# Order of the moving columns and place of the stationary buffers in a split-fp32 encoder trunk

## The chip, the cores and the metric

The kernel runs on one NeuronCore of a Trainium2 chip. The metric is device time of one launch in microseconds; 3 runs of the kernel before gave 2326.38, 2326.87 and 2327.36 us (median 2326.87).

## What is computed

One layer of an encoder trunk on 256 tokens of width 2048: half a SwiGLU FFN (width 5632), a mixing block in which a Conformer convolution (31 taps) and a 16-head latent attention work on the same normalised input and are merged by sigmoid gates, and a second half SwiGLU FFN. In outline:

```
x = x + 0.5 * swiglu_ffn(rms_norm(x, ffn1_norm_g), ffn1_w_gate, ffn1_w_up, ffn1_w_down)
u = rms_norm(x, mix_norm_g) @ w_in
y_conv = conformer_conv_branch(u_conv, ...) ; y_mla = mla_branch(c_q_raw, c_kv_raw, k_rope_raw, ...)
x = x + (sigmoid(gl_conv) * y_conv + sigmoid(gl_mla) * y_mla) @ w_out
x = x + 0.5 * swiglu_ffn(rms_norm(x, ffn2_norm_g), ffn2_w_gate, ffn2_w_up, ffn2_w_down)
return rms_norm(x, final_norm_g)
```

All of it is float32. The matrix products are by far the largest part, and nearly all are activations (256 tokens) times a weight matrix that is used once.

## The kernel before

**Units.** The weight matrices come from HBM in 814 units, one DMA each, issued by SyncE (L399). A unit of the wide stages holds two blocks (`DEEP = 2`) of 128 input channels by 512 output channels (`WIDE`), side by side in a partition: 128 partitions by 1024 floats. The host lays the weights out this way (`units_of`). 774 units are of this kind; 8 (the last group of the stage "latents") have blocks of 320 columns, and 32 belong to the attention heads, whose weights are laid out by another function (`head_units`).

**Rings.** A unit lands in one of four slots (`SLOTS`) of the ring `raw`. ScalarE rounds it to the reduced format fp32r into the ring `w_hi` (L432), VectorE writes the rest, raw minus rounded, into the ring `w_lo` (L927), and TensorE then multiplies. Activations are split into two such parts too and are kept whole in stationary buffers: `h`, `hidden`, `attn`, `merged`, `c_q` and `c_kv`.

**Products.** `wide_unit` does 12 matmuls for each unit: two blocks, two halves of the tokens, and three products each (`multiply`, L682 to L684: high by high, high by low, low by high). The stationary operand of each, loaded into the array by a LDWEIGHTS of its own, is 128 channels by 128 tokens of a stationary buffer; the moving operand is a block of 512 columns of `w_hi` or `w_lo`, read from the first column to the last; the result adds up in a PSUM bank. TensorE frees a slot with the last matmul of a unit (`unit_used`), and the three engines otherwise follow one another through counters (`hi_ready`, `lo_ready`), four units deep. In `head_pair` the queries and keys are made with the ring's weights as the stationary operand and `c_q` or `c_kv` moving (256 columns), the values with `c_kv` stationary and 256 columns of the ring moving. Attention scores and values (L799, L800, L825) and transposes (L693, L810, L879) are plain float32.

**Places.** In each partition the buffers lie one behind the other in the order in which they are declared. In the kernel before `w_hi` begins at byte 17536 and `w_lo` at 33920; `h` begins at 66688, `hidden` at 113792, `attn` and `merged` at 132224, `c_kv` at 197760 and `c_q` at 205952. Each of these is a multiple of 1024 bytes away from the others. A slot is 4096 bytes, a block of 512 columns 2048 bytes, a stationary block of 128 tokens 512 bytes.

Of the kernel before, what the change touches and what calls it, by code (L numbers as in the profile page):

```python
# [14 lines left out]
P = 128  # L15
# [19 lines left out]
WIDE = 512  # L35
DEEP = 2
SLOTS = 4
UNIT = WIDE * DEEP

AHEAD = SLOTS  # L40

# [122 lines left out]
def encoder(nc, streams, xt_in, x_in, pos_in, gains_in, final_in, taps_in, const_in, freq_in, out):  # L164
# [6 lines left out]
    with ExitStack() as ctx:  # L171
        def sb(name, shape, dt=F32, stack=ctx):
            return stack.enter_context(nc.sbuf_tensor(name, shape, dt))

        def sem(name):
            return ctx.enter_context(nc.semaphore(name))

        raw = sb("raw", [P, SLOTS, UNIT])
        w_hi = sb("w_hi", [P, SLOTS, UNIT], F32R)
        w_lo = sb("w_lo", [P, SLOTS, UNIT], F32R)  # L180
        x = sb("x", [P, 2, D])
        h = sb("h", [P, KT, 2, T], F32R)
        identity = sb("identity", [P, P])
# [91 lines left out]

        raw_loaded = [sem(f"raw_loaded{j}") for j in range(SLOTS)]
        xt_loaded = [sem(f"xt_loaded{j}") for j in range(KT // DEEP)]
# [60 lines left out]
        def banks(g):  # L338
            return bank[2 * g.pair], bank[2 * g.pair + 1]
# [51 lines left out]
        block = ctx.enter_context(nc.Block())  # L391

        @block.sync
        def _(sp):
            def load(u):
                stage, at, n = units[u]
                if u >= SLOTS:
                    sp.wait_ge(lo_ready, u + 1 - SLOTS)
# [278 lines left out]
        def _(pe):  # L677

            def multiply(dst, fixed, moving, first, last):
                fixed_hi, fixed_lo = fixed  # L680
                moving_hi, moving_lo = moving
                pe.matmul(dst, fixed_hi, moving_hi, start=first, stop=False)  # L682
                pe.matmul(dst, fixed_hi, moving_lo, start=False, stop=False)  # L683
                return pe.matmul(dst, fixed_lo, moving_hi, start=False, stop=last)  # L684
# [42 lines left out]
            def low_turned(stage, kinds, k):  # L727

                g = [g for g in plan.stage(stage) if g.kind in kinds][k // 4]
                t = turns[g.turn + k % 4 // 2]  # L730
                return t.lo_before + t.lo
# [19 lines left out]
            def wait_stationary(g, k):  # L751

                if g.stage == "ffn1_up":
                    pe.wait_ge(xt_lo, k + 2)
                elif g.stage in ("ffn1_down", "ffn2_down"):
                    pe.wait_ge(turn_lo, low_turned(g.stage[:4] + "_up", ("up",), k))
                elif g.stage == "conv_in":
                    pe.wait_ge(turn_lo, low_turned("ffn1_down", ("resid",), k))
                elif g.stage == "q_rope":
                    t = turns[plan.q_turn]  # L760
                    pe.wait_ge(turn_lo, t.lo_before + t.lo)
                elif g.stage == "mla_out":
                    pe.wait_ge(head_lo, k + 2)
                elif g.stage == "conv_out":
                    pe.wait_ge(ln_lo, k // 2 + 1)
                elif g.stage == "w_out":
                    pe.wait_ge(turn_lo, low_turned("conv_out", ("merge",), k))
                elif g.stage == "ffn2_up":
                    pe.wait_ge(turn_lo, low_turned("w_out", ("resid",), k))

            def wide_unit(u, g):
                fixed = STATIONARY[g.stage]
                slot, w = u % SLOTS, g.width
                pe.wait_ge(lo_ready, u + 1)
                if g is plan.stage(g.stage)[0]:
                    wait_stationary(g, DEEP * (u - g.u0))
                for r in range(DEEP):
                    k = DEEP * (u - g.u0) + r
                    moving = w_hi[:, slot, r * w:(r + 1) * w], w_lo[:, slot, r * w:(r + 1) * w]
                    for tt in range(2):  # L780
                        tokens = slice(tt * P, (tt + 1) * P)
                        last = multiply(banks(g)[tt][:, 0:w], (fixed[:, k, 0, tokens], fixed[:, k, 1, tokens]), moving,
                                        k == 0, k == g.deep - 1)
                last.then_inc(unit_used, 1)
# [103 lines left out]
            while u < n_units:  # L888
                if H0 <= u < M0:
                    head_pair((u - H0) // 4)  # L890
                    u += 4
                    continue
                if u == M0:
                    attend_scores(PAIRS - 1)
                if u in plan.starts:
                    wait_banks(plan.starts[u])
                    g = groups[plan.starts[u]]
                wide_unit(u, g)
                turn_after(u)
                if u == Q_END + LATE_TURN_AFTER:  # L900
                    late_turns()
                if u == M0:
                    attend_values(PAIRS - 2)
                if u == M0 + 3:
                    attend_turn(PAIRS - 1)
                if u == M0 + 4:
                    attend_values(PAIRS - 1)
                if FORE <= u < FORE + 8:
                    fore(u - FORE)
                if BACK <= u < BACK + 8:  # L910
                    back(u - BACK)
                u += 1
# [343 lines left out]

def units_of(w):

    k, width = w.shape
    return w.reshape(k // (DEEP * P), DEEP, P, width).transpose(0, 2, 1, 3).reshape(-1, P, DEEP * width)  # L1260


def column_groups(*weights):

    cuts = range(0, weights[0].shape[1], WIDE)
    return np.concatenate([units_of(w[:, c:c + WIDE]) for c in cuts for w in weights], 0)
# [85 lines left out]
```

## Time and profile before

| | us |
|---|---|
| median of 3 runs | 2326.87 |
| the profiled execution | 2326.71 |
| its span | 2324.8 |
| TensorE busy (matmul) | 2299.0 |
| TensorE weight loads, beside the matmuls | 1924.4 |
| VectorE busy | 1322.2 |
| ScalarE busy | 1188.3 |

The span runs from the first to the last instruction of the program; 1.9 us of the execution lie around it. A matmul's record reaches from its start to its modelled end, so the records of matmuls that follow each other overlap; how fast they follow is read from the distance between their starts. Weight loads have records of their own beside the matmuls.

### The profile page before, as it was taken

To read this page: it belongs to the slowest core of one execution; us is meant where nothing else is said; L and a number is where in the kernel's file an instruction comes from. 1 tells how busy PE (TensorE), PEld (TensorE's weight loads), DVE (VectorE), ACT (ScalarE), POOL (GpSimd) and SP (SyncE) were. 2 spreads that over 40 slices of the span, in tenths; PEclk is the share of its full clock that TensorE was granted. 3 is DMA by queue.
4 is the path that set the end of the run, shared out by engine and by line. 5 is a ranking of instruction groups with operands and counts; after the bars stand their busy time and mean duration, and the time that the engine had idled before them with its cause. 6 is when DMAs were issued, how large, how long until landed. Compare 5 with 4: busy or idle time off the path is not lost.

```text
span 2324.8 us, 26788 instructions
## 1 busy us (share of the span) xinstructions
PE 2299.0 (99%) x10718; PEld 1924.4 (83%) x10718; DVE 1322.2 (57%) x1470; ACT 1188.3 (51%) x1620; POOL 0.2 (0%) x4
## 2 busy tenths in 40 slices
PE   8999999999999999999999999999999999999997
PEld 7888888888888888878889888888888888888886
DVE  5544544544545488997875465555544544544443
ACT  6444444444444577787776564444444444444443
POOL 0000000000000000000000000000000000000000
PEclk9999999999999999999999999999999999999999
DMA  8666666666665665566643455656666666666664
GB/s 289 189 190 190 190 185 196 190 187 192 190 191 187 186 199 183 171 198 182 199 136 119 138 174 185 189 184 208 188 186 196 191 186 189 191 188 193 195 191 135
DMA packets 121532, 432.65 MB, mean 186 GB/s; under 512 B 13632, under 2 KB 13888, under 8 KB 121280
## 3 DMA queue, kind: packets, MB, share of 16 engines
q1 hardware_dynamic: 121408, 430.93, 60.0%
q8 instruction: 85, 1.39, 0.3%
q14 instruction: 39, 0.32, 0.0%
HBM read 428.78 MB, written 2.10 MB: 185 GB/s over the span
## 4 chain that ended last, share of the span: by engine, by line
PE 97%; DVE 1%; ACT 1%; issue 1%; DMA 0%; SPq 0%; ACTq 0%; DVEq 0%
PE bank L682 31%; PE bank L684 31%; PE bank L683 31%; PE turned L693 2%; PE bank L825 1%; PE bank L799 1%; PE bank L800 1%; DVE q_rope L1117 0%; PE turned L810 0%; ACT w_hi L432 0%; DVE w_lo L927 0%; DVE q_rope L1123 0%; DMA raw<-in_ffn_up 0%; PE turned L879 0%; ACT q_rope L540 0%
## 5 line engine op out<-in xcount | busy, mean ns | idle before, releaser
L927 DVE TENSOR_TENSOR w_lo<-raw,w_hi 128x1024 fp32r<-128x1024 f32 (+2 forms) x814 | 986.9, 1215 | 954.8 <-ACT w_hi L432 954.5
L432 ACT ACTIVATE w_hi<-raw 128x1024 fp32r<-128x1024 f32 (+2 forms) x814 | 853.0, 1051 | 998.4 <-PE bank L684 987.9
L682 PE MATMUL bank<-w_hi,h 128*128 128x512 f32 (+1 forms) x2144 | 835.9, 390 | 10.1 <-DVE w_lo L927 10.1
L684 PE MATMUL bank<-w_hi,h 128*128 128x512 f32 (+1 forms) x2144 | 832.7, 388 | 0.0
L683 PE MATMUL bank<-w_lo,h 128*128 128x512 f32 (+1 forms) x2144 | 832.6, 388 | 0.0
L682 PEld LDWEIGHTS bank<-w_hi,h 128*128 128x128 f32 x2144 | 403.0, 188 | 92.7 <-DVE w_lo L927 11.4
L684 PEld LDWEIGHTS bank<-w_hi,h 128*128 128x128 f32 x2144 | 402.9, 188 | 83.1
L683 PEld LDWEIGHTS bank<-w_lo,h 128*128 128x128 f32 x2144 | 403.1, 188 | 81.6
L682 PE MATMUL bank<-w_hi,hidden 128*128 128x512 f32 x704 | 274.3, 390 | 0.0
L684 PE MATMUL bank<-w_hi,hidden 128*128 128x512 f32 x704 | 273.9, 389 | 0.0
L683 PE MATMUL bank<-w_lo,hidden 128*128 128x512 f32 x704 | 273.9, 389 | 0.0
L684 PEld LDWEIGHTS bank<-w_hi,hidden 128*128 128x128 f32 x704 | 132.1, 188 | 27.5
L682 PEld LDWEIGHTS bank<-w_hi,hidden 128*128 128x128 f32 x704 | 132.1, 188 | 27.4
L683 PEld LDWEIGHTS bank<-w_lo,hidden 128*128 128x128 f32 x704 | 132.2, 188 | 27.2
L540 ACT ACTIVATE q_rope<-padded,taps 128x256 f32<-128x256 f32 x320 | 135.7, 498 | 1.0 <-DVE q_rope L1117 1.0
L1117 DVE TENSOR_TENSOR q_rope<-q_rope 128x1024 f32<-128x1024 f32 x76 | 92.6, 1218 | 0.0
L1123 DVE SCALAR_TENSOR_TENSOR q_rope<-padded,taps,q_rope 128x256 f32<-128x256 f32 x160 | 66.7, 479 | 0.0
L459 ACT ACTIVATE opened<-bank,rstd 128x512 f32<-128x512 f32 x52 | 33.0, 685 | 37.4 <-PE bank L684 37.4
L682 PE MATMUL bank<-w_hi,attn 128*128 128x512 f32 x128 | 52.0, 407 | 0.0
L682 PE MATMUL bank<-w_hi,merged 128*128 128x512 f32 x128 | 50.2, 392 | 0.0
L684 PE MATMUL bank<-w_hi,attn 128*128 128x512 f32 x128 | 50.1, 392 | 0.0
L683 PE MATMUL bank<-w_lo,attn 128*128 128x512 f32 x128 | 49.9, 390 | 0.0
(171 smaller groups left out, 1223.4 us busy)
## 6 DMA issues: line engine op xcount, KB each, us to landing
raw<-in_ffn_up SPq DMA_DIRECT2D x352, 512.0 KB, 4.1
raw<-in_ffn_down SPq DMA_DIRECT2D x176, 512.0 KB, 3.6
raw<-in_conv_in SPq DMA_DIRECT2D x64, 512.0 KB, 3.8
raw<-in_conv_gate SPq DMA_DIRECT2D x32, 512.0 KB, 4.2
raw<-in_mla_gate SPq DMA_DIRECT2D x32, 512.0 KB, 4.2
raw<-in_mla_out SPq DMA_DIRECT2D x32, 512.0 KB, 3.6
raw<-in_conv_out SPq DMA_DIRECT2D x32, 512.0 KB, 3.7
raw<-in_w_out SPq DMA_DIRECT2D x32, 512.0 KB, 3.6
```

The lines of the kernel that those rows point to most:

```text
L432: act.activation(w_hi[:, j, 0:n], raw[:, j, 0:n], ACT.Copy).then_inc(hi_ready, 1)
L459: act.activation(opened[:, tt, :], banks(g)[tt][:, :], func, scale=rstd[:, tt:tt + 1]).then_inc(by_act, 1)
L540: act.activation(conv_prod[made % 2][:, r, :], padded[:, m, t:t + T], ACT.Copy, scale=taps[:, m, t:t + 1]).then_inc(tap_made, 1)
L682: pe.matmul(dst, fixed_hi, moving_hi, start=first, stop=False)
L683: pe.matmul(dst, fixed_hi, moving_lo, start=False, stop=False)
L684: return pe.matmul(dst, fixed_lo, moving_hi, start=False, stop=last)
L693: last = pe.transpose(turned_bank[n % 2][:, r * T + tt * P:r * T + (tt + 1) * P], src[:, tt, c:c + P], identity[:, :])
L799: pe.matmul(dst, q_nope[:, j, cols], k_nope[:, j, :], start=True, stop=False)
L800: last = pe.matmul(dst, q_rope[:, p, 0, cols], k_rope[:, j, :], start=False, stop=True)
L927: dve.tensor_tensor(w_lo[:, j, 0:n], raw[:, j, 0:n], w_hi[:, j, 0:n], ALU.subtract).then_inc(lo_ready, 1)
L1117: dve.tensor_tensor(dst, conv_acc, conv_prod[made % 2], ALU.add).then_inc(tap_done, 1)
L1123: dve.scalar_tensor_tensor(out=conv_acc[:, r, :], in0=padded[:, m, t:t + T], scalar=taps[:, m, t:t + 1], in1=conv_acc[:, r, :], op0=ALU.mu ...
```

## The change

The moving operand of the wide stages is read in another order, the host lays the columns out so that the same columns come in the same order as before, and a pad of 192 bytes is put behind the rings.

```diff
+RUN = 16
 UNIT = WIDE * DEEP
...
         w_lo = sb("w_lo", [P, SLOTS, UNIT], F32R)
+
+        sb("after_weights", [P, 48])
         x = sb("x", [P, 2, D])
...
+            def in_turns(block):
+
+                return block.rearrange("p (h n t) -> p n h t", h=2, t=RUN)[:, ::-1, :, :]
+
             def wide_unit(u, g):
...
-                    moving = w_hi[:, slot, r * w:(r + 1) * w], w_lo[:, slot, r * w:(r + 1) * w]
+                    moving = in_turns(w_hi[:, slot, r * w:(r + 1) * w]), in_turns(w_lo[:, slot, r * w:(r + 1) * w])
...
 def units_of(w):
 
+
     k, width = w.shape
+    w = w.reshape(k, width // (2 * RUN), 2, RUN)[:, ::-1].transpose(0, 2, 1, 3)
     return w.reshape(k // (DEEP * P), DEEP, P, width).transpose(0, 2, 1, 3).reshape(-1, P, DEEP * width)
```

A block of 512 columns is seen as two halves of 256 (1024 bytes apart), each of 16 runs of 16 columns (64 bytes). The matmul reads the last run of the first half, the last run of the second half, then the run before in each, and so on down to the first ones; within a run it reads upwards. A block of 320 columns is read likewise, in 10 runs of each half. With the pad every buffer behind `w_lo`, and with them all stationary buffers, lies 192 bytes further on, which is a multiple of 256 less 64. `head_units` and `head_pair` are not changed.

## Rows read from the trace of the kernel before

**Rows 1.** The page's head and its busy times (share of the span) by engine.

```profile
span 2324.8 us, 26788 instructions
PE 2299.0 (99%) x10718; PEld 1924.4 (83%) x10718; DVE 1322.2 (57%) x1470; ACT 1188.3 (51%) x1620; POOL 0.2 (0%) x4
```

**Rows 2.** The page's chain of work that ended last: share by engine.

```profile
PE 97%; DVE 1%; ACT 1%; issue 1%; DMA 0%; SPq 0%; ACTq 0%; DVEq 0%
```

**Rows 3.** Groups of instructions, shapes apart: busy us, mean ns, idle before.

```profile
L927 DVE TENSOR_TENSOR w_lo<-raw,w_hi 128x1024 fp32r<-128x1024 f32 x790 | 965.4, 1225 | 926.7 <-ACT w_hi L432 926.4
L432 ACT ACTIVATE w_hi<-raw 128x1024 fp32r<-128x1024 f32 x790 | 833.8, 1059 | 988.3 <-PE bank L684 977.9 <-DMA raw<-in_ffn_up 5.8 <-DMA raw<-in_mla_out 1.4
L682 PE MATMUL bank<-w_hi,h 128*128 128x512 f32 x2112 | 826.0, 391 | 10.1 <-DVE w_lo L927 10.1
...
L682 PE MATMUL bank<-w_hi,hidden 128*128 128x512 f32 x704 | 274.3, 390 | 0.0
...
L682 PE MATMUL bank<-w_hi,attn 128*128 128x512 f32 x128 | 52.0, 407 | 0.0
L682 PE MATMUL bank<-w_hi,merged 128*128 128x512 f32 x128 | 50.2, 392 | 0.0
```

**Rows 4.** Timeline of TensorE in the first FFN: start us, us, instruction.

```profile
300.13 0.39 PE L682 MATMUL bank<-w_hi,h 128*128 128x512 f32 x1
...
302.85 0.39 PE L682 MATMUL bank<-w_hi,h 128*128 128x512 f32 x1
```

**Rows 5.** Timeline of the group whose blocks have 320 columns.

```profile
968.05 0.31 PE L683 MATMUL bank<-w_lo,h 128*128 128x320 f32 x1
...
975.09 0.31 PE L683 MATMUL bank<-w_lo,h 128*128 128x320 f32 x1
```

**Rows 6.** Timeline of the heads: 256 columns in fp32r, then the float32 scores.

```profile
1182.64 0.28 PE L684 MATMUL bank<-w_hi,c_kv 128*128 128x256 f32 x1
...
1185.16 0.28 PE L684 MATMUL bank<-w_hi,c_kv 128*128 128x256 f32 x1
1185.28 0.60 PE L799 MATMUL bank<-k_nope,q_nope 128*128 128x256 f32 x2
...
1188.31 0.59 PE L800 MATMUL bank<-k_rope,q_rope 128*128 128x256 f32 x2
```

**Rows 7.** Timeline of the heads after float32 matmuls: the first twelve in fp32r.

```profile
1290.48 0.47 PE L682 MATMUL bank<-c_q,w_hi 128*128 128x256 f32 x1
1290.79 0.28 PE L683 MATMUL bank<-c_q,w_hi 128*128 128x256 f32 x1
...
1291.62 0.28 PE L684 MATMUL bank<-c_q,w_lo 128*128 128x256 f32 x1
...
1292.22 0.28 PE L683 MATMUL bank<-c_q,w_hi 128*128 128x256 f32 x1
```

**Rows 8.** Instructions on the tiles `w_lo` and `identity`: duration ns min/median/max.

```profile
L683 PEld LDWEIGHTS bank<-w_lo,h x2144: 187/188/333, 8.3 to 2070.6; 128*128 128x128 f32 x195
L683 PE MATMUL bank<-w_lo,c_q x24: 387/389/389, 1157.3 to 1173.9; 128*128 128x512 f32 x24
...
L693 PEld LDWEIGHTS turned<-identity,prod x232: 139/140/146, 59.2 to 2077.3; 128*128 128x128 f32 x116
```

**Rows 9.** The page's DMA issues of the FFN weights.

```profile
raw<-in_ffn_up SPq DMA_DIRECT2D x352, 512.0 KB, 4.1
```

**Rows 10.** Busy us by engine, convolution stretch and steady stretch: clock, DMA share, GB/s.

```profile
924.00:1050.00 126.00, 124.08 (x593) 104.44 (x593) 114.92 (x165) 102.48 (x187) 0.00 (x0) 1.00 0.60 185
1700.00:1900.00 200.00, 200.00 (x904) 166.03 (x903) 99.63 (x90) 85.37 (x89) 0.00 (x0) 1.00 0.62 191
```

## The prediction

> **What bounds the kernel now.** I read the page's head first. TensorE is busy for 2299.0 of 2324.8 us [rows 1], and the chain that ended last lies on it for 97% [rows 2]. The groups say the same from the other side: ScalarE's rounding sits idle for 988.3 us, nearly all of it until a matmul frees a slot, and VectorE waits in turn for ScalarE; TensorE's costliest group waits for VectorE only 10.1 us in all [rows 3]. So the time is the number of matmuls times the distance between their starts, and only a change of that distance moves it much.
>
> The timeline gives the distance. From 300.13 to 302.85 us there are twelve steps, so a matmul of 512 columns starts every 2.72 / 12 = 226.67 ns [rows 4]. With 320 columns 48 steps take 975.09 - 968.05 = 7.04 us, 146.67 ns each [rows 5]; with 256 columns 21 steps take 1185.16 - 1182.64 = 2.52 us, 120.0 ns each [rows 6]. The slope between 256 and 512 columns is 106.67 / 256 = 0.4167 ns a column, one cycle at 2.4 GHz, which is the granted clock (1.00) [rows 10]. What is left is the same for all three: 226.67 - 213.33 = 13.33 ns, 146.67 - 133.33 = 13.33, 120.0 - 106.67 = 13.33, or 32 columns' time. The change can only aim at these 13.33 ns, 5.9% of a wide matmul.
>
> Is it a fixed price of a matmul with its own weights? Two rows say no. The float32 scores also load weights for each record, and 14 of their records (7 steps of two) take 1188.31 - 1185.28 = 3.03 us, 216.4 ns each [rows 6]. That is the time of 512 columns plus only 3.1 ns. They stream 256 columns in it, one in two cycles, so their moving operand asks memory for half as much per ns. And right after such a stretch the fp32r matmuls do not start at 120.0: seven steps from 1290.79 to 1291.62 take 118.6 ns each, then five to 1292.22 take 120.0 [rows 7]. Same operands, same places, another distance until the loads and the streams have found a fixed rhythm. A load also lasts 188 ns beside an fp32r stream but 140 beside a float32 transpose [rows 8]. I read all three as two read streams, the moving operand and the next stationary one, that get into each other's way by timing.
>
> **The change, part by part.** *Order and pad.* In a steady stretch a load of 128 columns is repeated every 120 ns [rows 6], so it takes at most 120 / 8 = 15 ns for each 16 columns (64 bytes); the moving operand takes 226.67 / 32 = 7.1 ns for a run of 16. Two moving runs, one from each half, thus take about as long as one run of the load. The two halves are 1024 bytes apart, so if the memory's parts repeat every 256 or 1024 bytes both runs lie in one part, and the moving stream steps down by 64 bytes at about the pace at which a load walks. If the load walks down too (from its last column, which no row shows), the two never meet, given a right starting distance, which the 64 bytes set. Before, the stream walks up at twice the pace and crosses the load again and again, at a cost independent of the block, as rows 4 to 6 show. All stationary buffers lie at one distance from the rings modulo 1024, so the trace cannot show what another distance would cost; the pace argument is what I go by.
>
> The value: the remainder of a wide matmul falls from 13.33 to the 3.1 ns of the scores, 10.24 ns less. There are 774 x 12 = 9288 wide matmuls: 3 x 2112 on h, 3 x 704 on hidden, 3 x 128 on attn and on merged, 3 x 24 on c_q [rows 3, 8]. 9288 x 10.24 ns = 95.1 us, and 96 matmuls of 320 columns give 1.0. Bounds: 0 ns left gives 9288 x 13.33 = -123.8 us; nothing gained gives 0; on the bad side a seam between runs can cost time (a rival below). I take the scores' 3.1 ns since they are the nearest fp32 stream beside loads that is not slowed.
>
> [...]
>
> *Heads.* 84 matmuls of 256 columns for each of 8 head pairs, 672 in all, keep their order, but c_q and c_kv move by 64 bytes against the rings. Taken at nothing. Below: they go to the 118.6 ns of rows 7, 672 x -1.4 = -0.9 us; above: the 13.33 ns double, +9 us.
>
> *VectorE and ScalarE.* Their operands are the same in size and contiguous, only shifted; 0. A faster TensorE however takes a unit in 12 x 216.4 = 2.60 us instead of 2.72. The rounding (1059 ns) and the split (1225 ns) have room for that in the steady stretch, where VectorE is busy 99.63 of 200 us. Not between 924 and 1050 us, where convolution taps are due and VectorE is busy 114.92 of 126 us, TensorE already short of 1.9 [rows 3, 10]. Some 550 of the 593 matmuls there would save 5.6 us; VectorE would then have to be busy 114.92 of 120.4, 95%. I let half of it be lost: +3 us (0 to +5.6). What waits there is the next unit's split, queued behind the taps on VectorE, and TensorE behind it.
>
> *DMA.* Same 512 KB units, landing in 4.1 us [rows 9] against four slots of 2.60 us; 0.62 of the DMA engines' time becomes 0.65 [rows 10]. Nothing; if this cover went, the price would be what the queue is short of, and nothing shows that.
>
> *The sum.* 2326.71 (the profiled execution, 0.16 under the median) - 95.1 - 1.0 + 3 = 2233.6 us; I say **2234**.
>
> **The rivals.**
> *Partly cleared.* The rhythm that sets in still lets some reads collide, a quarter to three quarters of the 13.33 ns remaining above the floor. For it: the system finds its own rhythm, as rows 7 show, and the 64 bytes fit one starting distance only. With half of the gain, 48 us, the time is 2279; the case spans 2252 to 2310.
>
> *No change.* The 13.33 ns are paid for each load however the addresses lie. For: they are the same for w on either side of the product and three widths, to 0.1 ns. Against: rows 6 and 7 as above. The time stays 2326 to 2328. [...]
>
> *Slower: the seams.* The moving operand becomes 32 runs of 64 bytes with a jump back and forth of 1 KB, where it was one sweep. If each of 32 seams costs one cycle, 0.4167 ns, that is +13.33 ns for each wide matmul; with the collisions gone the net is +3.1 ns, 9288 x 3.1 = +29 us, 2356; with collisions kept +124 us, 2451. It decides from 10.24 / 32 = 0.32 ns a seam. For it: no matmul in the trace has a moving pattern of more than one run, so nothing bounds it. Against: each run is 64 aligned bytes, and the next address is known far ahead. The same place ends far worse if the equal pace makes the streams stay on one part of the memory instead of avoiding each other: every 16-column step of the load then collides, and a time above 2400 is possible.
>
> **How the numbers follow.** Cleared as in the sum 0.47 (2222 to 2246), partly cleared 0.24, no change 0.11, slower 0.18. Partly cleared lies wholly on the faster side. From this faster 0.71, same 0.11, slower 0.18; 0.2% of the time is 4.7 us, about what a measurement of this kernel tells from no change. The range runs from 2212, where most of the 3.1 ns would be gone too, to 2329, so that it takes in partly cleared and no change and leaves out the seams (0.18) and the full 13.33 ns.
>
> **What would show it.** Right: starts 216 to 217 ns apart in the FFN stages, weight loads under 188 ns, heads at 120 ns, TensorE waiting for VectorE a few us more around 924 to 1050 us, a DMA share of 0.65. A distance of 226.67 in the FFN says that the 13.33 ns are a fixed price; 217 to 225 that the rhythm only partly avoids collisions; above 227 that seams or a worse meeting cost. If the distance falls as said but the time by much less, the bound has moved to VectorE, and its idle time before the split is gone.

## The result and the profile after

The changed kernel takes 2339.21 us (median of 5 runs, 2338.0 to 2339.53) against 2326.87 (5 runs): ratio 1.0052, 95% interval 1.0037 to 1.0067. It is slower by 12.3 us. I had forecast 2234 us and a range that ended at 2329.

TensorE is still the bound; the page's head and chain answer to [rows 1, 2].

```profile
span 2337.7 us, 26788 instructions
...
PE 2311.6 (99%) x10718; PEld 1919.9 (82%) x10718; DVE 1321.8 (57%) x1470; ACT 1187.0 (51%) x1620; POOL 0.2 (0%) x4
...
PE 97%; DVE 1%; ACT 1%; issue 1%; DMA 0%; SPq 0%; ACTq 0%; DVEq 0%
```

The groups, shapes apart, answer to [rows 3]: the same counts, ScalarE and VectorE idle a little longer, TensorE waiting for VectorE as before.

```profile
L935 DVE TENSOR_TENSOR w_lo<-raw,w_hi 128x1024 fp32r<-128x1024 f32 x790 | 964.9, 1224 | 939.1 <-ACT w_hi L436 938.9
...
L686 PE MATMUL bank<-w_hi,h 128*128 128x512 f32 x2112 | 827.0, 392 | 10.0 <-DVE w_lo L935 10.0
```

The timeline of TensorE, in the first FFN and in the first head pair (start us, us, instruction), answers to [rows 4, 6].

```profile
300.11 0.39 PE L688 MATMUL bank<-w_hi,h 128*128 128x512 f32 x1
...
302.85 0.39 PE L688 MATMUL bank<-w_hi,h 128*128 128x512 f32 x1
...
1183.26 0.28 PE L688 MATMUL bank<-c_q,w_lo 128*128 128x256 f32 x1
...
1186.66 0.28 PE L688 MATMUL bank<-c_q,w_lo 128*128 128x256 f32 x1
```

Twelve wide matmuls take 2.74 us, 228.3 ns each, where it was 226.67. Thirty head matmuls take 3.40 us, 113.3 ns each, where it was 120.0; in other head pairs it is 117.8. Over the whole trace the mean distance of the wide ones went from 226.88 to 228.49 ns (without gaps of 300 ns and more) and of the head ones from 119.8 to 117.0. 9288 x 1.61 ns = +15.0 us and 672 x -2.8 ns = -1.9 us give +13.1; the span grew by 12.9. So within 0.2 us the whole result is in the distance of the starts, and nothing went elsewhere.

### The profile page after: what moved, and what is told of

Its sections match the earlier page's. It is cut to its first block, busy times and chain, and to the rows that moved or that the text cites. A ratio compares the mean times of both kernels' runs of the same rounds, so it can differ in the third digit from the quotient of the medians.

```text
span 2337.7 us, 26788 instructions
## 1 busy us (share of the span) xinstructions
PE 2311.6 (99%) x10718; PEld 1919.9 (82%) x10718; DVE 1321.8 (57%) x1470; ACT 1187.0 (51%) x1620; POOL 0.2 (0%) x4
## 4 chain that ended last, share of the span: by engine, by line
PE 97%; DVE 1%; ACT 1%; issue 1%; DMA 0%; SPq 0%; ACTq 0%; DVEq 0%
PE bank L686 31%; PE bank L688 31%; PE bank L687 31%; PE turned L697 2%; PE bank L833 1%; PE bank L807 1%; PE bank L808 1%; DVE q_rope L1125 0%; PE turned L818 0%; ACT w_hi L436 0%; DVE w_lo L935 0%; DVE q_rope L1131 0%; DMA raw<-in_ffn_up 0%; PE turned L887 0%; ACT q_rope L544 0%
```

## The experiments

**The two halves of the change.** Each alone, then the pad with other sizes. e1 is the kernel before plus

```diff
+        sb("after_weights", [P, 48])
```

> The 192-byte pad alone, columns read in one sweep as before. Theory (the loads of the stationary operand and the moving stream collide, and the 32 columns' time depends on their distance in memory): the heads, which keep their one sweep and got only the new place, went from 120.0 to about 117.8 ns a matmul in the changed kernel; if the wide matmuls gain the same 2.2 ns, 9288 x 2.2 = 20 us, about 2306 us, starts 224.4 ns apart in the FFN. Rival (the 13.33 ns are a price of each load in the wide matmuls, and the change's 12 us are seams of the new order): 2327 us, 226.7 ns.

Measured: 2344.74 us, ratio 1.0077 (1.0064 to 1.0091); the wide matmuls are 228.96 ns apart, the heads 117.0. Both theories miss: the pad does change the wide matmuls, but for the worse, while it helps the heads. Twelve steps in the first FFN, 2.75 us or 229.2 ns each:

```profile
299.82 0.39 PE L686 MATMUL bank<-w_hi,h 128*128 128x512 f32 x1
...
302.57 0.39 PE L686 MATMUL bank<-w_hi,h 128*128 128x512 f32 x1
```

e2 is the changed kernel less that line.

> The new order alone, without the pad. Theory (place decides): a time that differs from the changed kernel's 2339 us by more than 5 us either way; if the seams cost a fixed sum and the place gives 2.2 ns as in the heads, 228.4 + 2.2 = 230.6 ns a wide matmul and 2360 us. Rival (place is nothing in the wide matmuls, the order costs its 1.7 ns alone): 2339 us, 228.4 ns.

Measured: 2384.92 us, ratio 1.0245 (1.0231 to 1.0259); the heads at 119.8 ns as before. In the trace, whose execution took 2379.56 us, 708 wide units run without a gap of 250 ns or more: 550 at 233.3 to 233.6 ns and 158 at 230.0, nearly all of these before 572 us. Place decides, also for the new order, and more than I expected. Of +58 us for the order the pad takes back 46: the two parts do not add up, they act together.

**A sweep of places and orders.** A kernel that does no layer: in each of its 80 settings 36 matmuls with the kernel's three products, on three blocks of the rings, with the stationary operand in a buffer `room`. A distance of 0 is the kernel before's, a multiple of 1024 bytes from the rings; the others lie so many bytes further on. The figures are the mean from one start to the next, from the 13th start on.

> A sweep and nothing of the layer: 36 fp32r matmuls of 512 columns with the kernel's way of products for each of 80 settings of order and of the stationary operand's place against the rings, two float32 matmuls between settings. Calibration: one sweep at distance 0 gives 226.7 ns, the new order at 192 bytes 228.3. Theory (collisions by place and time): the distance of starts varies with the place by several ns, repeats with a fixed number of bytes, and with 96, 64, 32 and 1 columns of stationary operand the rest above 213.3 ns falls in proportion to about 3 ns. If the new order can avoid the load at all, some place gives under 218 ns. Rival (a price of each load, and seams): the same 13.3 ns at every place and for every number of stationary columns, and the new order 1.7 ns above it everywhere.

Measured, ns from start to start, 512 columns:

```
distance of stationary operand, bytes:   0     64    128    192    256 ...
one sweep                              226.7  233.4  232.3  228.8  226.7
the change's order                     233.4* 226.7  228.4  228.2  230.0*
all runs of the block, last run first  233.4  233.4  236.8  237.7  233.3
the change's order, run order upwards  240.0  240.0  239.9  240.0  240.0
every column backwards                 233.4  233.4  233.3  233.4  233.3
columns loaded (one sweep, 0):    128: 226.7   96: 230.0   64: 229.8   32: 231.7   1: 229.1
```

The pattern repeats every 256 bytes, up to 960. The very first setting (one sweep, 0) averages 227.7 and settles at the 226.7 that 256, 512 and 768 bytes give. The starred pair is one place with two rhythms, the same two as in e2. Distances of 16, 32 and 48 bytes, too, give 233.3 to 233.4 ns for one sweep and 233.2 to 233.4 for the change's order. With other lengths of the runs, at 192 bytes, the change's order gives 251.0 (4 columns), 245.2 (8) and 236.6 (32). The timeline (three settings: one sweep at 256, one sweep at 64, one column loaded) shows how such a number is read: 24, 24 and 26 steps.

```profile
64.11 0.39 PE L120 MATMUL bank<-w_hi,room 128*128 128x512 f32 x1
...
69.55 0.39 PE L120 MATMUL bank<-w_hi,room 128*128 128x512 f32 x1
...
73.00 0.40 PE L121 MATMUL bank<-w_lo,room 128*128 128x512 f32 x1
...
78.60 0.40 PE L121 MATMUL bank<-w_lo,room 128*128 128x512 f32 x1
...
522.71 0.40 PE L120 MATMUL bank<-w_hi,room 128*1 128x512 f32 x1
...
528.66 0.39 PE L122 MATMUL bank<-w_hi,room 128*1 128x512 f32 x1
```

5.44 / 24 = 226.7, 5.60 / 24 = 233.3, and 5.95 / 26 = 228.8. Both readings in my expectation fell in part. Place counts, with a period; but the rest above 213.3 ns does not shrink with a shorter load, so it is not paid for the load's length. A load of one column, whose record lasts 82 ns instead of 188, even stands higher (229.1) than one of 128 (226.7). And no place or order of these at 512 columns lies below 226.6.

**Back to the kernel.** e3 is the changed kernel with `sb("after_weights", [P, 16])`, a distance of 64 bytes.

> The new order with a pad of 64 bytes in place of 192. The sweep gave 226.65 ns for this order at a distance of 64 bytes, as for one sweep at 0. Theory (the place of the stationary buffers modulo 256 sets the rhythm, and 32 columns' time is the least that either order reaches): starts 226.7 ns apart in the FFN and a time of 2322 to 2332 us, about 12 us under the changed kernel. Rival (the sweep's rhythm does not carry over, since SyncE, ScalarE and VectorE use the memory beside TensorE in the kernel): 2339 us or more.

Measured: 2330.58 us, ratio 1.0017 (1.0008 to 1.0026). Of the 708 wide units without a gap 669 stand at 226.7 ns, and 35 at 236.7, a rhythm that the sweep had not shown. It is as expected, within the band, and 8.6 us under the changed kernel. It is still 4.1 us slower than the kernel before, and the 35 units account for that: 35 x 12 x 10 ns = 4.2 us.

e4 has one sweep and `sb("after_weights", [P, 64])`.

> A pad of 256 bytes, columns in one sweep. Theory (the pattern repeats every 256 bytes): as before, 2327 us, 226.7 ns in the FFN. Rival (a pad as such costs, or a longer period): 2340 us or more.

Measured: 2326.6 us, ratio 1.0000 (0.9990 to 1.0009), 226.88 ns as before. A pad as such costs nothing, and the kernel agrees with a period of 256.

e6 has one sweep and `sb("after_weights", [P, 16])`: the worst place of its row in the table.

> A pad of 64 bytes, columns in one sweep. The sweep gave 233.43 ns for one sweep at 64 bytes. Theory (the sweep's table holds in the kernel): 9288 x 6.76 ns = +62.8 us, less 1.5 in the heads, 2388 us, units at 233.3 to 233.5 ns. Rival (nothing but the order costs, places are worth a ns or two): under 2350 us.

Measured: 2384.86 us, ratio 1.0250 (1.0231 to 1.0269), 233.34 ns. The table forecasts the kernel to 3 us. Twelve steps take 2.80 us, 233.3 ns each:

```profile
299.83 0.39 PE L685 MATMUL bank<-w_lo,h 128*128 128x512 f32 x1
...
302.63 0.39 PE L685 MATMUL bank<-w_lo,h 128*128 128x512 f32 x1
```

**What pays the price.** The second sweep changes types, widths, the load's walk and PSUM's use.

> A second sweep, nothing of the layer: fewer columns, the new order with fewer columns, a stationary operand of every 2nd column, sums spread over banks or none, bf16 and float32 operands, the low ring moved against the high one, and all loads from one place. Theory now (since one-column loads did not lower the distance: the price is paid where one fp32r stream with a load beside it gives way to the next, not for the length of the load): 13.3 ns or more above the columns' time for every number of columns in fp32r at distance 0, a place-dependent part of up to 7 ns, and 2.5 to 3 ns for bf16 and float32 at every place. Rival 1 (the price is the load's own, whatever the type): bf16 also 13.3 ns. Rival 2 (PSUM's adding up costs it): 2.5 ns when each matmul starts anew. Rival 3 (the load's reads collide after all): a load of every 2nd column changes the distance by several ns, and loads all from one place too.

Measured: bf16 at 215.83 ns at all four distances and with the change's order, float32 (256 columns, two records each) at 215.83 a record for either order; spread over two banks or each sum started anew, fp32r stays at 226.7 (one sweep) and 228.4 (the change's order); a load of every 2nd column gives 235.6, 230.0, 231.3 and 233.2 for one sweep and 234 to 240 for the new order. Merged rows of the timeline, bf16 in one sweep and in the change's order:

```profile
323.72 7.50 PE L163 MATMUL bank<-w_b,room_b 128*128 128x512 bf16 x34
...
364.79 7.50 PE L163 MATMUL bank<-w_b,room_b 128*128 128x512 bf16 x34
```

33 steps and one record of 0.38 us: (7.50 - 0.38) / 33 = 215.8 ns, for 32 runs as for one sweep. So 32 seams cost nothing in bf16, and none in fp32r either where the change's order stands at 226.7 ns like one sweep (64 bytes, and e3). My slower rival falls in its form of a fixed price for each seam; why runs of 4 and 8 columns stand at 251.0 and 245.2 was not looked into. Where a matmul's sum goes in PSUM plays no part that shows (226.7 and 228.4 ns, as against 226.7 and 228.2 in the first sweep). Of the streams tried, fp32r, whose 512 columns are 2048 bytes of a partition in 226.7 ns, pays; bf16 reads 1024 bytes in 215.83 ns, and a float32 record grows from 111.7 to 215.83 ns between 128 and 256 columns, 0.81 ns a column where fp32r has 0.4167. Rival 3 is right as far as it goes: how the load walks matters (235.6 against 226.7 ns at distance 0). The type theory holds for distance 0; the fewer columns do not: 256 gave 120.0, 320 146.7 and 384 173.3 ns at distance 0, but 448 gave 202.7 (199.9 at 192 bytes), and 192 and 128 are slower than their columns by 31.5 and 160 ns. And for 256 columns 120.0 is not the least: 117.7 to 118.9 ns at the other three distances. One more figure bears on the prediction: the loads of the float32 streams last 190 to 192 ns in these settings, no less than the 188 beside fp32r, although these streams are not slowed.

The third sweep sorts the moving columns by place modulo 256.

> A third sweep, nothing of the layer. Known so far: bf16 and float32 stand at 215.8 ns at every place and order, fp32r at 226.7 to 240 by place and order; 226.7 is the least seen with 128 columns loaded. Theory (load and stream meet in parts of the memory of 64 bytes that repeat every 256): with 'load spread' (every column of the load in the same 64 bytes modulo 256) and the moving columns sorted by place (by_place: 128 columns of each part in turn, so the first half of the matmul, in which the load runs, stays in two of the four parts), two of the four distances are free of meetings and stand clearly lower than the other two, by 5 ns or more, and by_place_down swaps them. If meetings were all of the price, the free ones would stand at 216 to 218. Rival (a fixed price of 13.3 ns at the hand-over between two full-rate streams, over which meetings only add): the free ones stand at 226.7 and nothing of the 49 settings with 512 columns goes below 226.6. One-column loads from one place: the same at both distances for each order (a one-column load has nothing to meet).

Measured: none of the settings called by_place (128 columns of one 64-byte part, then of the next) was low; 239.7, 243.3, 245.5 and 241.5 ns with the load spread, and 240 to 243 for by_place_down. The theory's clean pairs did not come, so two of four parts is no refuge: a stream that stays long in one part is slow by itself (238.4 ns with one column loaded, at both distances). The rival's floor held: nothing below 226.65. That the load runs in the first half of the matmul, as the expectation has it, was an assumption: its records last 295 to 308 ns in these settings, longer than the step from one start to the next. What did come is an identity. Groups of 256 bytes taken last first with upward runs gave at all four distances the figures of one sweep (226.7, 233.4, 232.3, 228.8), and upward groups with downward runs those of "all runs of the block, last run first" (233.3, 233.4, 236.8, 237.7): in these orders only an address modulo 256 counts. One-column loads came out the same at both distances for three of five orders, but 229.1 and 231.6 for one sweep.

So the fourth sweep holds the stream and the load still, each in one 64-byte part modulo 256.

> A fourth sweep, nothing of the layer: the moving operand reads the same 64 bytes 32 times over (or the same 16, 128 or 256 bytes), the load stays in one 64-byte part modulo 256 (load spread), walks 512 bytes, or is one column. Theory (stream and load meet only where they are in the same 64-byte part modulo 256; a fixed hand-over price beneath): with the stream in part p and the load spread in part d, the diagonal p = d stands higher by 5 ns or more and the 12 others stand alike, at 226.7 if the 13.3 ns are a fixed price, at 216 if they were meetings. Rival (no such parts; what counts is the time at which a stream or a load crosses a boundary of 64 or 256 bytes): no diagonal; all 16 alike, since neither stream nor load changes its part, and the same for one column. If the stream's own walk through memory is what costs 13.3 ns, all the 64-byte settings stand near 216, and the 256-byte ones at 226.7.

Measured, ns, with the load spread in one part:

```
stream reads the same 64 bytes of part   0     1      2      3
load in part 0                          275  243.4  243.4  243.4
load in part 1                         243.4  273.4  243.4  243.4
load in part 2                         243.3  243.4  273.1  243.4
load in part 3                         243.4  243.4  243.4  273.3
stream in part 0, one column loaded: 243.4 at all four; load of 512 bytes: 240.0  242.2  238.1  240.1
stream over the same 16 bytes of part 0: 216.6 to 216.9 with each of the three kinds of load
stream over 128 bytes, parts 0 and 1, load in part 0, 1, 2, 3: 240.0  244.5  235.6  235.6
stream over the same 256 bytes, load in part 0, 1, 2, 3: 233.4  233.4  240.0  233.4
stream over the same 256 bytes, load of 512 bytes: 226.7 at distance 0, 233.4 at 64
```

The rows are, in order: stream and load both in part 1; stream in part 1 and load in part 2; stream over the same 16 bytes (the names `w_hi` and `w_lo` alternate as in the kernel); and a weight load of the first and of the second setting.

```profile
90.42 0.44 PE L164 MATMUL bank<-w_lo,room 128*128 128x512 f32 x1
...
93.70 0.44 PE L164 MATMUL bank<-w_lo,room 128*128 128x512 f32 x1
...
122.91 0.41 PE L164 MATMUL bank<-w_lo,room 128*128 128x512 f32 x1
...
126.56 0.41 PE L164 MATMUL bank<-w_lo,room 128*128 128x512 f32 x1
...
253.34 0.38 PE L164 MATMUL bank<-w_lo,room 128*128 128x512 f32 x1
...
256.58 0.38 PE L164 MATMUL bank<-w_lo,room 128*128 128x512 f32 x1
...
90.97 0.34 PEld L164 LDWEIGHTS bank<-w_lo,room 128*128 128x128 f32 x1
...
124.13 0.29 PEld L164 LDWEIGHTS bank<-w_lo,room 128*128 128x128 f32 x1
```

3.28 / 12 = 273.3, 3.65 / 15 = 243.3 and 3.24 / 15 = 216 ns. The diagonal is the answer on meetings: a load that stays in the stream's own part costs 30 ns, in any other nothing. Such a load is not the kernel's: its record lasts 292 ns against 188, and 342 on the diagonal, so these runs do not separate a stream that gives way from a matmul that waits for a longer load. The kernel's kind of load, which walks 512 bytes and has a quarter of them in the stream's part, adds nothing to 243.4 (238.1 to 242.2). But the price beneath is not the load's. It is 30 ns (243.4 - 213.3) when the stream reads the 64 bytes of one part over and over, with the load in another part or down to one column, and 25 to 29 with the walking load; 13.3 when it goes through all four parts at the best distance; and 3 when it reads the same 16 bytes over and over, even with the load in its own part. The theory's diagonal is right and its fixed hand-over price wrong; the rival without parts is wrong. The last reading in the expectation, that the stream's own walk costs the 13.3 ns, fails as I had put it (the 64-byte streams are not near 216). But how far the stream walks does count: 216.6 ns over the same 16 bytes, 243.4 over the same 64; no run has a stretch between the two. One figure does not fit an account by addresses modulo 256 alone: with the load in part 1, one sweep through the whole block stands at 237.9 ns (third sweep), the same 256 bytes again and again at 233.4.

**Best of both.** Only the heads gained from 192 bytes, so e5 gives the distance to them and to the 72 wide matmuls on c_q alone.

```diff
+        sb("before_c_kv", [P, 48])
         c_kv = sb("c_kv", [P, KVT, 2, T], F32R)
```

> The kernel before with 192 bytes of pad in front of c_kv and c_q alone: the wide stages keep distance 0 (226.7 ns), only the heads (and the 72 wide matmuls on c_q) get the distance of the changed kernel. Theory (place sets the rhythm of each stream and load pair by itself): heads at 116.7 to 117.8 ns instead of 120.0, wide stages 226.7; 672 x -2.6 + 72 x 2.2 ns = -1.6 us, 2325 us. Rival (the heads' gain comes from something else in the changed kernel): 120.0 ns and 2327 us.

Measured: 2325.26 us against 2326.52, ratio 0.9994 (0.9985 to 1.0003). The trace has the heads at 116.9 ns and the wide units at 226.89, as expected. The rows are eighteen steps, 2.12 us or 117.8 ns each on average, in a head pair.

```profile
1289.87 0.28 PE L684 MATMUL bank<-c_q,w_hi 128*128 128x256 f32 x1
...
1291.99 0.28 PE L684 MATMUL bank<-c_kv,w_hi 128*128 128x256 f32 x1
```

The rhythm is shown; that the kernel is faster is not, since the interval holds 1. Its median is the lowest of all versions.

## Why the prediction was wrong, step by step

- *The bound* was right: TensorE by the distance of starts, 32 columns' time over the columns in rows 4 to 6, and all but 0.2 us of the result lies there. The 2.4 GHz is the slope put the other way, 1 / 0.4167 ns; the trace gives the granted clock only as a share of full speed, 1.00.
- *The reading of rows 6 to 8* went one step too far. They show that the fp32r stream pays for something that a float32 stream does not; I took all of it for meetings with the load. But 13.3 ns for a sweep through all parts remain with the load cut to one column (229.1 ns, no less) and stood under every setting of the four sweeps with 512 fp32r columns that did not read the same 16 bytes over and over. The 188 against 140 ns of rows 8 said nothing on it, and the trace of before could have told me: the scores, whose stream I called not slowed, have loads of 190 ns themselves, as the float32 streams of the second sweep have.

```profile
L799 PEld LDWEIGHTS bank<-k_nope,q_nope x64: 186/190/192, 1185.2 to 1302.1; 128*128 128x128 f32 x64
```

- *Order and pad*, the term of -95.1 us, is the step that failed. "The remainder falls from 13.33 to the 3.1 ns of the scores" assumed that the load causes the remainder and that an order can avoid it. The runs show in its place that the remainder stays with next to no load beside the stream (229.1 ns with one column loaded), and that the kernel before already stood on the least value that any order or place tried reached at 512 columns, 13.33; every other one tied or raised it. By the change it rose to 15.2, +15.0 us. That none could lie lower is not shown. The scores, whose 3.1 ns I took as the floor, take 216.4 / 256 = 0.85 ns a column, a wide matmul 226.67 / 512 = 0.44. Their loads last as long (190 ns), and an fp32r stream over the same 16 bytes stands at 216.6 to 216.9 ns under any of three kinds of load; so the loads are not what sets the scores apart. What fits is how fast a stream comes to bytes that it has not just read: 2048 of a partition in 226.7 ns in fp32r, 1024 in 215.8 in bf16 and in a float32 record of 256 columns, none after the first 16 at 216.6. That this is the cause is an estimate from these figures and was not isolated.
- The geometry behind the change was half right. Parts of 64 bytes that repeat every 256 are real, and a meeting with a load that stays in one costs 30 ns (fourth sweep, 273.3 against 243.4); that the 0 to 7 ns of place in the kernel are such meetings is argued, not shown. Within the new order the distance matters as I argued that it must, 226.7 at 64 bytes against 230 to 233 at 0. But 192 bytes is not its best distance: 228.2. At 64 the order only ties with one sweep at 0, and in the kernel it is 4.1 us slower.
- *Heads*: taken at nothing, bounds -0.9 to +9 us; measured -1.9. They came below my bound, as 118.6 ns was a mean of a passing rhythm and 113.3 was there to be had. So for 256 columns the 13.3 ns are no floor: 6.7 were left at best, half of what there was, by place alone.
- *VectorE's +3 us* was the price of a speed-up that did not come, and stays untested. DMA: nothing, as said; its share between 1700 and 1900 us is 0.63, where it was 0.62.
- *The rivals.* "No change" was right for the larger share, in that no order tried removed it at 512 columns; that the load is what is paid for fails on one-column loads (229.1 ns), and it left no room for place. "Seams" at a fixed price each is refuted by bf16, 215.83 ns in 32 runs as in one, and by e3. "Partly cleared" needed a floor under 13.3; besides, a quarter to three quarters of the 13.33 ns above the 3.1 would have been 2262 to 2324 us, not 2252 to 2310. The sign that came true, slower, is nearest to what I had only named in a sentence and priced above 2400 us: a worse place for stream and load. e2 and e6, at 2385 us, show that price nearly whole.
- What I should have asked of the trace of before: whether 120.0, 146.67 and 226.67 ns, all exactly 32 columns over, were the mark of an undisturbed rhythm and not of a disturbed one. In rows 7 the passing rhythm was faster than the settled one, which misled me.

**What stays open.** Why an fp32r stream pays 30 ns in one part and about 16 in four (243.4 and 229.1 ns) with next to no load beside it, and why a load of 128 columns stands lower than one of a single column; why 256 columns can go below 13.3 ns and 512 did not; why some places have two rhythms (230.0 and 233.3 ns; 113.3 and 117.8), and what picks one; and what the by_place orders and the runs of 4 and 8 columns pay for. An fp32r stream with no load at all was not tried.

## What to carry to other kernels

Before you move operands to avoid a conflict, measure the price with the suspected partner taken away: a sweep of 80 settings in one short kernel foretold e4 and e6 to about 3 us and e3 to within 5. Where TensorE streams 512 columns of fp32r in one sweep, keep the stationary buffers a multiple of 256 bytes from the moving rings (226.7 ns at 256, 512 and 768); a pad of 64 bytes cost this kernel 58 us, and in the sweep 16 bytes raise a matmul as much as 64 (233.4 ns). For 256 columns try the other distances too: 192 bytes took the heads from 119.8 to 117.0 ns. A fixed remainder in the distance of starts is no proof of a conflict that can be scheduled away; compare it with other types on the same operands, not with other instructions of the kernel.

## What the runs showed of the hardware that I had not expected

- fp32r matmuls of 512 columns start 226.7 to 251 ns apart in the orders and places tried, up to 273 to 275 when stream and load stay in one part; bf16, and float32 with 256 columns for each record, stand at 215.8.
- One sweep stands at 226.7 ns with the load 256, 512 or 768 bytes away and at 233.4 at 64, 320, 576 or 832: addresses act modulo 256 bytes there. For a load that stays in one of four parts of 64 bytes, the stream's own part costs 30 ns a matmul (273.3 against 243.4). A stream over the 64 bytes of one part stands 30 ns above its columns' time with one column loaded (243.4 against 213.3), and one over the same 16 bytes 3 (216.6).
- A stream of 32 runs with jumps of 1 KB costs nothing as such: 215.83 ns in bf16, and 226.7 in fp32r at the best distance, as in one sweep.
- 128 columns of fp32r take 213.3 ns, as long as 512 columns at 0.4167 ns each, and 192 take 111.6, less than 128.
